# The opening of a two-layer encoder kernel: adaLN sums moved to TensorE, three weight slabs fed tile by tile, and arrays laid out by the host

## The reference

```
def adaln(c, w, b):
    mod = (c @ w + b)[:, None, :]
    shift, scale, gate = jnp.split(mod, 3, axis=-1)
    return shift, scale, gate
...
    for l in range(DEPTH):
        shift, scale, gate = adaln(c, w_ada_mix[l], b_ada_mix[l])
        u = x * (1.0 + scale) + shift
        y = hybrid_mixer(u, w_in[l], conv_w[l], conv_b[l], conv_ln_g[l], conv_ln_b[l],
                         sinks[l], w_out[l], cos, sin)
        x = layer_norm(DN_ALPHA * x + (1.0 + gate) * y, ln1_g[l], ln1_b[l])
        shift, scale, gate = adaln(c, w_ada_ffn[l], b_ada_ffn[l])
        u = x * (1.0 + scale) + shift
        y = conv_gated_mlp(u, w_up[l], ffn_conv_w[l], ffn_conv_b[l], w_down[l])
        x = layer_norm(DN_ALPHA * x + (1.0 + gate) * y, ln2_g[l], ln2_b[l])
```

## Time and profile before

| | |
|---|---|
| median of 3 runs | 2102.32 us (2102.18 to 2103.11) |
| the profiled execution | 2101.31 us |
| its span in the trace | 2099.5 us |
| PE busy | 2064.8 us (98%) |
| PEld busy | 1701.8 us (81%) |
| POOL busy | 1413.6 us (67%) |
| DVE busy | 1191.1 us (57%) |
| ACT busy | 1031.2 us (49%) |

### The profile page before, as it was taken

The page is one execution under the profiler, slowest core; times in us unless marked ns, Lnnn a source line. Parts: engine busy times, 40 slices in busy tenths (PEclk is TensorE's granted clock), DMA queues, the critical chain, the costliest instruction groups (busy, mean ns, idle before and its releaser), DMA issues.

```text
span 2099.5 us, 27374 instructions
## 1 busy us (share of the span) xinstructions
PE 2064.8 (98%) x9619; PEld 1701.8 (81%) x9619; DVE 1191.1 (57%) x1940; ACT 1031.2 (49%) x1845; POOL 1413.6 (67%) x1780
## 2 busy tenths in 40 slices
PE   7999999999999999999999999999999999999997
PEld 6877778787888878888788888888878888888887
DVE  5888888675515554777632645587651455332235
ACT  3585356555516674374643756235562465333332
POOL 4987767755778887875557885564556776545454
PEclk9999999999999999999999999999999999999999
DMA  8644544533434354553233333332323332434332
GB/s 301 157 134 148 161 127 148 162 108 103 121 111 124 107 162 145 141 159 93 76 100 106 111 111 91 101 103 73 100 76 107 88 104 84 128 99 123 94 100 78
DMA packets 421510, 250.07 MB, mean 119 GB/s; under 512 B 48149, under 2 KB 393085, under 8 KB 421373
## 3 DMA queue, kind: packets, MB, share of 16 engines
q1 hardware_dynamic: 420506, 248.03, 39.8%
q10 hardware_dynamic: 867, 0.29, 0.1%
HBM read 242.71 MB, written 4.26 MB: 118 GB/s over the span
## 4 chain that ended last, share of the span: by engine, by line
PE 86%; POOL 5%; ACT 3%; DVE 3%; issue 2%; ACTq 0%; DMA 0%; POOLq 0%; DVEq 0%
PE fg L886 27%; PE fg L888 27%; PE fg L887 27%; POOL w_lo L1932 3%; PE bank_s L984 1%; POOL ada_acc L2003 1%; ACT ada L1324 1%; PE bank_l L915 1%; PE bank_t L993 1%; PE bank_t L1006 1%; DVE bank_c L1539 0%; POOL ssum L2030 0%; POOL u_lo L2012 0%; ACT probs L1291 0%; ACT probs L1283 0%
## 5 line engine op out<-in xcount | busy, mean ns | idle before, releaser
L1932 POOL TENSOR_TENSOR w_lo<-raw,w_hi 128x256 fp32r<-128x256 f32 (+1 forms) x1425 | 1031.3, 755 | 609.8 <-ACT w_hi L1163 608.7
L886 PE MATMUL fg<-u_hi,w_hi 128*128 128x512 f32 x2112 | 834.7, 395 | 6.2 <-DVE u_lo L1519 2.6
L888 PE MATMUL fg<-u_hi,w_lo 128*128 128x512 f32 x2112 | 823.7, 390 | 0.0
L887 PE MATMUL fg<-u_lo,w_hi 128*128 128x512 f32 x2112 | 823.5, 390 | 0.0
L1163 ACT ACTIVATE w_hi<-raw 128x1024 fp32r<-128x1024 f32 (+2 forms) x387 | 375.6, 971 | 385.6 <-PE fg L888 278.4
L886 PEld LDWEIGHTS fg<-u_hi,w_hi 128*128 128x128 f32 x2112 | 397.1, 188 | 102.5 <-issue 14.5
L888 PEld LDWEIGHTS fg<-u_hi,w_lo 128*128 128x128 f32 x2112 | 397.0, 188 | 84.2
L887 PEld LDWEIGHTS fg<-u_lo,w_hi 128*128 128x128 f32 x2112 | 397.4, 188 | 80.1 <-issue 0.5
L1539 DVE SCALAR_TENSOR_TENSOR bank_c<-glu,par,bank_c 128x512 f32<-128x512 f32 x448 | 306.1, 747 | 0.1
L1886 DVE SCALAR_TENSOR_TENSOR x<-fg,mod,x 128x512 f32<-128x512 f32 (+1 forms) x168 | 121.6, 724 | 319.3 <-PE fg L888 319.0
L888 PE MATMUL fg<-h_hi,w_lo 128*128 128x512 f32 (+1 forms) x704 | 269.8, 383 | 0.0
(11 more groups left out here) (272 smaller groups left out, 1860.8 us busy)
## 6 DMA issues: line engine op xcount, KB each, us to landing
raw<-in_w_up_dram SPq DMA_DIRECT2D x176, 512.0 KB, 3.8
ada<-in_w_ada_ffn_dram SPq DMA_DIRECT2D x48, 512.0 KB, 4.4
raw<-in_w_down_dram SPq DMA_DIRECT2D x64, 384.0 KB, 3.5
raw<-in_w_in_dram SPq DMA_DIRECT2D x40, 512.0 KB, 4.0
raw<-in_w_down_dram SPq DMA_DIRECT2D x64, 320.0 KB, 3.1
ada<-in_w_ada_mix_dram SPq DMA_DIRECT2D x32, 512.0 KB, 4.2
raw<-in_w_in_dram SPq DMA_DIRECT2D x32, 256.0 KB, 3.7
raw<-in_w_out_dram SPq DMA_DIRECT2D x32, 256.0 KB, 2.9
```

Source lines behind the costliest of these rows:

```text
L886: pe.matmul(out, hi[:, k, :], rhi, start=k == order[0], stop=False)
L887: pe.matmul(out, hi[:, k, :], rlo, start=False, stop=False)
L888: ins = pe.matmul(out, lo[:, k, :], rhi, start=False, stop=k == order[-1])
L1932: ins = pool.tensor_tensor(lo_of(n)[:, ks, :], raw[n % NRAW][:, ks, :], hi_of(n)[:, ks, :].bitcast(F32), ALU.subtract)
```

## The change

The host hands over `x` already transposed, the first adaLN weights packed in the order of use (`ada_first`, eight tiles of 1 MB, each in two halves: shift and scale), the other adaLN weights transposed (`ada_t`), and `c` as a column. It also puts the output together from two arrays, of which the first is stored as `x` lies, so that steps `xt` and `tm` go, and all transposes with them. The `idle_products` go too.

The first sums are now wholly PE's: `first_part(k)` makes shift and scale of feature tile k with 16 products of one column. Slabs 0, 1 and 2 (`g`, `a` of channel tile 0 and `g` of tile 1) run together, with nine matmuls of 512 columns for each feature tile, and one `first_part` between.

The later chunks: POOL multiplies by `c` (`c_rows`, which is `c` on every partition), two instructions of 128x512 for each part, and ACT adds up along the row as it copies (`accum_out`), one slab later (step `ae`); for chunks 8 to 10 DVE does it in one instruction. Step `as` goes.

```diff
-BANK = [n % 2 if n < FIRST_UP else (n + 2) % 3 for n in range(NSLAB)]
+BANK = [2 if n == 2 else n % 2 if n < FIRST_UP else (n + 2) % 3 for n in range(NSLAB)]
...
+            def first_part(k):
+                if k >= 2:
+                    pe.wait_ge(first_fold, 2 * (k - 1))
+                for half in (0, 1):
+                    pe.wait_ge(in_first[k][half], 16)
+                    for d in range(DT):
+                        ins = pe.matmul(bank_c[k % 2][:, half:half + 1], first_ada[k][:, half, d * P:(d + 1) * P], ccol[:, d:d + 1],
+                                        start=(half, d) == (0, 0), stop=(half, d) == (1, DT - 1))
+                ins.then_inc(first_sum, 1)
...
+                if ns[0] == 0:
+                    first_part(1)
                 for n in ns:
                     if n < NLOAD:
                         pe.wait_ge(lo_ready, n + 1)
...
                 for k in order:
+                    if ns[0] == 0 and 0 < k < DT - 1:
+                        first_part(k + 1)
...
-                    if ns[0] == 0 and k == DT // 2 - 1:
-                        first_rest()
+                    if ns[0] == 0 and k == DT - 1:
+                        taps_turn()
...
+            for half in (0, 1):
+                pe.matmul((bank_t, bank_s)[half][:], ones_1[0:1, :], c_rows[0:1, half, :], start=True, stop=True).then_inc(set_pe, 1)
             pe.wait_ge(in_const, 16 * IN_CONST)
             for l in range(DEPTH):
                 ins = pe.transpose(fg[1][:, l * P:l * P + N1], rows1[0:N1, l, :], ident[0:N1, 0:N1])
             ins.then_inc(set_pe, 1)
-            first_sums(0)
-            idle_products(12, fg[0])
+            pe.wait_ge(in_ccol, 16)
+            first_part(0)
             for n in range(NSLAB):
                 between = [step for step in STEPS[n - 1] if step in INSIDE] if n else []
-                if n in PAIRS:
+                if n == 0:
+                    slabs((0, 1, 2), between)
+                elif n in PAIRS:
...
+            split_hi(0)
             for k in range(DT):
-                if k == DT // 2:
-                    split_hi(2)
                 first_inputs(k)
-            act.wait_ge(set_pe, 4)
+                if k < 2:
+                    split_hi(k + 1)
+            act.wait_ge(set_pe, 5)
...
+            def first_fold_in(k):
+                dve.wait_ge(first_sum, k + 1)
...
-            for n, (p, k) in enumerate(FIRST_ADDS):
-                if n == FIRST_HALF:
-                    fold("half", 0)
-                add_first(n, p, k)
-            fold("half", 1)
...
+            dve.wait_ge(set_par, 1)
+            first_fold_in(0)
+            for k in range(DT):
+                if k + 1 < DT:
+                    first_fold_in(k + 1)
+                first_lo(k)
...
-            for n in range(2):
-                split_lo(n)
-            for k in range(DT // 2):
-                first_lo(k)
+            split_lo(0)
+            split_lo(1)
+            split_lo(2)
             angles(0)
-            split_lo(2)
-            pool.wait_ge(set_pe, 4)
+            angles(1)
+            pool.wait_ge(set_pe, 5)
             for j in range(CT):
                 history(0, j)
-            angles(1)
             split_lo(NHI)
```

More of the change, by code:

```diff
@@ L289, in plan @@
                 used[n] += 15
[L290 to L293 removed]
+        for part, n in enumerate(ns):
+            if c not in DVE_CHUNKS:
+                at(n + 1, "ae", c, part)
+        if c >= DVE_CHUNKS[0]:
+            used[ns[-1] + 2] += 7
     for n, what, i in ((18, "gate", 0), (47, "gate", 1), (100, "ss", 2), (145, "gate", 2), (165, "ss", 3),
@@ L1153, in _ @@
                 act.dma_start(pos[f * FBLK:(f + 1) * FBLK, :], turn[0]).then_inc(in_pos, 16)
-            for name, n in ROWS1:
-                load(rows1[OFF[name]:OFF[name] + n, :, :], a[name].rearrange("l (t p) -> t l p", p=P))
             def split_hi(n):
@@ L1820, in background @@
                 elif what == "ad":
-                    add_ada(*step[1:])
-                elif what == "as" and step[1] not in ONES_CHUNKS:
-                    reduce_ada(step[1])
+                    ada_total(*step[1:])
                 elif what == "fold":
```

439 lines of the change are left out of this document (128 added, 311 removed).

## The result

The changed kernel takes 2160.07 us (median of 4 runs, 2147.88 to 2163.93), the kernel before 2102.72 us beside it: a ratio of 1.026, with a 95% interval of 1.0218 to 1.0302. It is 2.6% slower, where 1.7% (2138 us) was forecast, and 10 us beyond the range. Its profiled execution took 2161.29 us, with a span of 2159.3.

The account below looks back on a forecast made before the run. PE was taken as the bound from 145 us, level with POOL from 57.7, waiting before. Slab 2's end (97.3) + 5.9 + 2.4 + 2041.8 - 12.3, plus 1.8 around it, gave 2136.9 us, median 2138; range 2106 to 2150.

Parts of the forecast that it names:

- The opening: Everything ahead of slab 3: slab 2 ends at 97.3 us and slab 3 starts near 103 us.
- Start: PE waits for `rows1`, then does two transposes; `first_part(0)` starts at 11.4 us.
- Parts: 16 single-column products: 3.28 us at full clock; at half, 3.28 to 6.4, the upper end taken.
- Wait on `u_lo`: PE waits 1.43 us behind each next part, because `u_lo` stands behind the next tile's gain and bias on DVE.
- Tile: Part, wait and nine slab matmuls in the opening: 10.1 us each, six such.
- Clock: Every burst of slab matmuls in the opening at half clock, half of the six parts behind a burst at full.
- To slab 3: Between slab 2 and slab 3, four transposes, then a chain on ACT and POOL up to `w_lo`, 5.4 us.
- From slab 3 on: Slab 3 to the end: 2041.8 us before, less 12.3 for removed PE work; 2.4 added for a half-clock start.
- Weight loads keep their pace: Rival, opening: parts stay 3.28 us at either clock, bursts at half; median 2123 us, chance 0.16.
- The clock holds: Rival, opening: steady single-column products keep or bring the full clock; median 2110 us, chance 0.20.
- Faster: Rival, opening: single-column products run at half the pace time shown, 1.64 us a part; median 2097 us, chance 0.05.
- The later gain stays away: Rival, after slab 3: POOL's 22 us more holds PE, so the 12.3 us are not gained; 2150 us, chance 0.07.

Follow-up runs that it names:

- m4_both: Changed kernel with POOL waiting between its adaLN multiplications, `u_lo` ahead of the next gain and bias, and `w_hi` of slabs 1 and 2 early: 2138.06 us.
- n1_light: m4_both with POOL's multiplications of the first two later chunks cut to one column: 2133.67 us.
- k1_gap: Changed kernel with POOL waiting for each of its own multiplications of the adaLN parts before going on: 2147.16 us.
- m1_thin: Changed kernel with 1 of the 8 single-column products of each first-layer sum, 112 of 128 left out: 2100.31 us.
- m2_psum: Changed kernel with first-layer sums on DVE instead of PE, `c` read from PSUM, POOL waiting between adaLN multiplications, `w_hi` 0 to 2 early: 2096.84 us.
- o1_logap: m2_psum with POOL's clears and first adaLN part early, plus POOL waits between all low-part pieces from slab 17 on: 2117.68 us.
- m3_sbuf: m2_psum with `c` read from SBUF and DVE instructions on whole rows of 1024: 2098.48 us.

## Why the prediction was right in sign and wrong in size

**The opening** came as forecast, in 3.7 us: slab 3 at 106.92 us for 103.2. *Start*: 13.80 us for 11.4; `rows1` landed later than their issue plus a landing gave. *Parts*: 6.82 us at half clock for 6.4, and 3.7 to 3.8 behind a burst that ended at full for 3.28. So the upper end was the right one to take, if low: twice 3.28 is 6.56, where the prediction has 6.4. *First wait*: 5.86 for 6.1. *Wait on `u_lo`*: 0.92 us six times for 1.43: the chain from the sums to `u_lo` was priced 0.5 us too long. *Tile*: 10.2 us (two in 20.4) for 10.1. *Clock*: bursts at half, every second part at full, as taken; that it came out so exactly is partly luck, since the number of parts at full differs between kernels with the same opening (m4_both and n1_light). *Transfers*: 11.5 MB at 352 GB/s are 33 us, not 35; they hid either way. *To slab 3*: 5.13 for 5.4.

**From slab 3 on** is the step that failed: "Before, this took 2041.8 us", with 12.3 us off and 2.4 for the half-clock start, came to 2031.9 us, and it took 2052.4, 20.5 us more. The gain was there, 15.3 us for 12.3. What the sum left out were losses of 25.9 us where it had 2.4, of three kinds. First, DVE instructions held beside POOL instructions without a gap, for which the sum had nothing: "Later POOL is idle for a third of the time, which hides the rest". They cost 12 to 13 us by k1_gap, with the clock that falls behind each new PE wait. Second, the stretch up to slab 14, for which the prediction said "I take nothing": it added 3.9 us from the start of slab 3, for 2.4 in the sum as the clock. The gain of the `xt` steps was given back by slab 11. Third, smaller jumps (slabs 24, 33, 35, 113, 133, 211, 385) that are left in k1_gap with 0.7 to 1.8 us each; these were not taken apart, and their cause is open.

The prediction priced POOL's new instructions as time on POOL, 22 us, and asked whether POOL had it. It didn't ask what their form does to DVE: the additions before waited for each other, the multiplications don't.

**The rivals.** *Weight loads keep their pace* fell: parts took 6.82 us at half clock. *The clock holds* fell, but m1_thin shows that it held with parts of 0.5 us. *Faster* needed that too. *The later gain stays away*, at 2150, was nearest in number and wrong in its reason: the gain came, and n1_light gives POOL's extra load of the first two chunks 2.7 us (that of the other fifteen was not tested by itself).

**The trade itself.** Before, the sums ran on DVE while PE had nothing it could do. The change puts them on PE: 128 products, 96 of them between the slab matmuls, and with them nearly every slab matmul of the opening at half clock. m2_psum shows that the other parts of the change (host layouts, three slabs fed tile by tile), with POOL's gap and the early `w_hi`, are worth having when the sums stay with DVE: 5.9 us below the kernel before. What each of them gives by itself was not tested.

## What to carry to other kernels

Before putting narrow products between wide ones on PE, price them at half clock, with the wide ones too; if another engine idles in that stretch, give it the sums. When an edit turns a chain of dependent POOL instructions into independent ones, look at DVE's small instructions with operands in SBUF beside them, and let POOL wait for itself once in a few microseconds; between all pieces it cost far more than it gave (o1_logap). And where work is taken from one engine in a stretch in which a second is level with it, ask for the second one's time per tile: the gain ends where the two meet.

## What was not expected of the hardware

- A DVE instruction of 4 columns, with its inputs in SBUF, was held for 9.10, 9.09 and 6.17 us over runs of POOL instructions that followed each other without a gap, and ones of 512 columns for 12.17 and 12.92 us; each of POOL's took 0.7 to 1.3 us. One wait of POOL on its own semaphore between two of them let it in (0.75 us). Not every such run holds DVE: one DVE instruction of 512 columns took 1.14 us amid one (m2_psum, 92.42 us).
- Where both engines had work without a break in m3_sbuf, neither was shut out: DVE 1.73 us for 1.26, POOL 1.35 us for some 0.73.
- Single-column fp32 products went at 0.21 us a record (13.67 us for 64) at half clock and at 0.12 a record (3.73 for 32) behind a burst that ended at full. Parts of 0.5 us between wide bursts of 2.1 us, with 0.92 us idle, left the clock at full; parts of 1.8 us did not.
- Waits of POOL between all four pieces of its low parts from slab 17 on, by which one low part took 3.25 us in place of 2.77, cost the kernel 21 us, in a stretch in which POOL is idle for a third of the time.
